# Weight remainders on GpSimd and three seven-product steps in every feed-forward chunk from the third

## The chip, the cores and the metric

One Trainium2 chip, one of its cores. The metric is the device time of one execution in microseconds (us), the median over several runs. Engines: TensorE (PE in the profile, PEld for its weight loads), VectorE (DVE), ScalarE (ACT), GpSimd (POOL), and SyncE (SP), whose queue issues nearly all weight loads.

## The reference

One layer of a decoder on 256 tokens of width 2048, in float32: `x + 1/2 SwiGLU`, `x + Mixer`, `x + 1/2 SwiGLU`, and a last RMSNorm. The change concerns the two feed-forward stages alone:

```python
def rmsnorm(x, g):
    y = x * lax.rsqrt(jnp.mean(x * x, axis=-1, keepdims=True) + EPS)
    return y * g
def swiglu(h, wg, wu, wd):              # wg, wu: 2048 x 5632, wd: 5632 x 2048
    return (jax.nn.silu(h @ wg) * (h @ wu)) @ wd
x = x + 0.5 * swiglu(rmsnorm(x, ffn1_norm), ffn1_wg, ffn1_wu, ffn1_wd)
x = x + hybrid_mixer(rmsnorm(x, mix_norm), ...)
x = x + 0.5 * swiglu(rmsnorm(x, ffn2_norm), ffn2_wg, ffn2_wu, ffn2_wd)
return rmsnorm(x, final_norm)
```

## The kernel before

**Precision.** Every float32 operand is split into a rounded high part and a remainder, both in a format that PE multiplies at full rate. A product is three matmuls: high x high, high x remainder, remainder x high. ScalarE makes the high part of a weight (`w_hi`, line 1305), VectorE the remainder (`w_lo <- raw - w_hi`, `lo`, line 1820).

**Slots.** Weights stream through four buffers. A slot `c` is one load of 512 KB (two k-tiles of 128 rows by 512 columns) into `raw[c % 4]`. ScalarE's `hi` waits until it has landed and until PE has finished slot c - 4; VectorE's `lo` follows; then PE's `group` does 12 matmuls of 128x512 (two k-tiles, two token tiles, three matmuls). SP loads slot c when slot c - 4 has its remainder (`lo_ready`) and, for a PAIR slot, when the weight sums of that step are made (`t_ready`). Each queue serves in order, and no queue skips a waiting instruction.

**Chunks.** A feed-forward stage f has 11 chunks n of 512 of the 5632 columns, 16 slots each: eight for the gate (wg), eight for up (wu). Chunks 0 to 5 are followed by the first part of the down projection, chunks 6 to 10 by the second. Gate results lie in PSUM banks 0 and 1 (one per token tile), up results in banks 2 and 3.

**Seven-product steps.** A PAIR slot (gate weights) and the PAIR2 slot behind it (up weights of the same k-tiles) form one step: the 2x2 block product of two token tiles, two k-tiles and the gate and up columns is done with seven products instead of eight, so with 21 matmuls instead of 24 (`seven_products`). For it VectorE forms four sums of weights in `wt` (`weight_sums`, lines 1882 to 1887), ScalarE splits them (`wt_hi`, line 1356) and VectorE makes their remainders (`wt_low`, line 1892); PAIR2's own remainder is needed for one k-tile only (line 1900). `weight_sums` waits until PE has finished the step before. Some products gather in PSUM banks 4 to 7 and are added to the four banks at the end of a chunk: `product1_copy` (ScalarE, line 1383) copies one bank to `z` when the last step is done, `gate_products` (lines 1957, 1942, 1944, 1959) adds to gate bank 0, forms two sums and adds to gate bank 1, `right_sums` (1950, 1952) forms the sums for up, and `up_products` (1965) adds them when all 16 slots are done.

**Tables.** `CHUNK` holds the slot order of a chunk with two steps, `CHUNK3` that of one with three (at slots 4, 8 and 12); `THREE` lists the chunks that use `CHUNK3`. For chunks in `LATE` the last step ends at slot 13, and the gate sums and SiLUs of chunk n - 1 are done within chunk n's program: ScalarE's `late_silu` behind slots 0 and 1, VectorE's `gate_products` behind slot 0, `right_sums` behind slot 1, `up_products` and `up` (line 2022: SiLU(gate) x up) behind slot 2, and the 32x32 transposes (`gu_transpose`, line 2066) behind slot 3. PE begins chunk n only when both SiLUs of chunk n - 1 have read the gate banks (`silu_done`). GpSimd then issues 16 small DMAs that complete the transposition (`gu_blocks`, line 712), and later slots (9, 10 and 14 with `CHUNK3`, 12 and 13 with `CHUNK`) make the operands of the down projection from them. GpSimd has no other work in these stages.

Of the kernel before, what the change touches and what calls it, by code (L numbers as in the profile page):

```python
# [14 lines left out]
NT = TOK // P  # L15
# [36 lines left out]
         (UP, 0), (UP, 1), (PAIR, 3), (PAIR2, 3), (UP, 4), (UP, 5), (UP, 6), (UP, 7)]  # L52
CHUNK3 = [(GATE, 0), (GATE, 4), (GATE, 5), (GATE, 6), (PAIR, 1), (PAIR2, 1), (GATE, 7), (UP, 0),
          (PAIR, 2), (PAIR2, 2), (UP, 4), (UP, 5), (PAIR, 3), (PAIR2, 3), (UP, 6), (UP, 7)]
THREE = (2, 4, 5, 6, 8, 10)
LATE = (0,) + THREE
H_QUAD = {1: 0, 2: 1, 3: 2}
PAIRS = 2
# [32 lines left out]
def chunk_slot(n):  # L91

    return CHUNK_SLOTS * n + (len(down_job(0)) if n >= PART0[1] else 0)
# [49 lines left out]
def job_no(f, key):  # L143

    return f * len(PAIR_JOBS) + PAIR_JOBS.index(key)
# [10 lines left out]
R_FFN1B, R_CONV, R_ATT, R_FFN2B = range(4)  # L156


def resid(stage, n):

    return NT * (stage * NDC + n + 1)
# [31 lines left out]
AT = {key: MIX0 + n for n, key in enumerate(MIX_ORDER)}  # L193
FFN0 = [0, MIX0 + len(MIX_ORDER)]
END = FFN0[1] + FFN_GROUPS
OUT0 = AT[("out", 1), 0]


# [88 lines left out]
def count(c, i=None, per=0):  # L287

    return c if i is None else i * per + c


def build_program(nc, a, out):
# [170 lines left out]
    with ctx:  # L463
# [3 lines left out]
        landed = [sem(f"landed{s}") for s in range(SLOTS)]  # L467
        hi_ready = sem("hi_ready")
        lo_ready = sem("lo_ready")
        group_done = sem("group_done")  # L470
        x_half_landed = sem("x_half_landed")
        w_half_landed = sem("w_half_landed")
# [126 lines left out]
        def _(sp):  # L599
            def load(c, src, halves=None):  # L600
                if c >= SLOTS:
                    sp.wait_ge(lo_ready, c - SLOTS + 1)
                for f in range(2):
                    if c - SLOTS - FFN0[f] in PAIR_SLOTS:
                        sp.wait_ge(t_ready, pair_no(f, c - SLOTS) + 1)
                s = c % SLOTS
                if halves is None:
                    sp.dma_start(raw[:, s, :, :], src).then_inc(landed[s], 16)
                else:
                    sp.dma_start(raw[:, s, :, 0:CMP_HID], halves[0]).then_inc(landed[s], 16)  # L610
                    sp.dma_start(raw[:, s, :, CMP_HID:CH], halves[1]).then_inc(landed[s], 16)
# [69 lines left out]
        def _(pool):  # L681
# [24 lines left out]
            def gu_blocks(f, n, i=None):  # L706
# [3 lines left out]
                for a_ in range(QB):  # L710
                    for c_ in range(QB):
                        pool.dma_start(gu_raw[c_ * SQ:c_ * SQ + SQ, :, a_, :],  # L712
                                       gu_sq[a_ * SQ:a_ * SQ + SQ, :, c_ * P:c_ * P + P]).then_inc(gu_moved, 16)

            def ffn(f):
                with pool.Fori(0, NFC - 1) as i:
                    gu_blocks(f, 0, i)
                gu_blocks(f, NFC - 1)

            ffn(0)  # L720
            pool.wait_ge(group_done, MIX0)
# [33 lines left out]
        def _(pe):  # L755
            mm = nc.tensor.matmul

            def group(c, i, per, hi, lo, k, banks, first, last, tiles=range(NT), signal=group_done, opened=(), skip=False):


                pe.wait_ge(lo_ready, count(c + 1, i, per))
                s = c % SLOTS
                for kk in range(GK):
                    for t, bank in enumerate(banks):
                        if t not in tiles:
                            continue
                        o = ps[:, bank, :]
                        x_hi = hi[:, k + kk, t * P:t * P + P]
                        x_lo = lo[:, k + kk, t * P:t * P + P]
                        begin = first and kk == 0 and t not in opened  # L770
                        mm(o, x_hi, w_hi[:, s, kk, :], start=begin, stop=False, skip_group_check=skip)  # L771
                        mm(o, x_hi, w_lo[:, s, kk, :], start=False, stop=False, skip_group_check=skip)  # L772
                        ins = mm(o, x_lo, w_hi[:, s, kk, :], start=False, stop=last and kk == GK - 1,  # L773
                                 skip_group_check=skip)
                if signal is not None:
                    ins.then_inc(signal, 1)
# [506 lines left out]
        def _(act):  # L1283
# [143 lines left out]
            def ffn(f):  # L1427
# [24 lines left out]
                def chunk(n, i=None):  # L1452
                    c = FFN0[f] + chunk_slot(n)
                    gu_at = 9 if n in THREE else 12
                    for p, (kind, _) in enumerate(chunk_table(n)):
                        slot(f, c + p, kind, i)
                        if n - 1 in LATE and n != PART0[1] and p < NT:
                            late_silu(f, n - 1, p)
                        if n == 1 and p == 8:
                            hs_high(f, 1)  # L1460
                        if n - 1 not in LATE and p == 0:
                            silu(f, n - 1, i, tiles=(1,))
                        if n != PART0[1]:
                            if p == gu_at:
                                gu_operand(f, n - 1, i)
                            if p == gu_at + 1:
                                gs_high(n - 1, quad_no(f, n - 1), i)
                        if n == PART0[1] and p == 0:
                            product1_copy(f, ("down", 0, 1), c - HALF[0] + last_pair(0, 1))
                        if p == 14 and n not in LATE:  # L1470
                            product1_copy(f, n, c + chunk_pairs(n)[-1], i)
                        if p == 15 and n not in LATE:
                            silu(f, n, i, tiles=(0,))
# [330 lines left out]
        def _(dve):  # L1804
# [10 lines left out]

            def lo(c, i=None, per=0):

                dve.wait_ge(hi_ready, count(c + 1, i, per))
                s = c % SLOTS
                tt(w_lo[:, s, :, :], raw[:, s, :, :], w_hi[:, s, :, :].bitcast(F32),  # L1820
                   ALU.subtract).then_inc(lo_ready, 1)
# [266 lines left out]
            def ffn(f):  # L2088
# [20 lines left out]
                def chunk(n, i=None):  # L2109
                    c = FFN0[f] + chunk_slot(n)  # L2110
                    gu_at = 9 if n in THREE else 12
                    for p, (kind, _) in enumerate(chunk_table(n)):
                        slot(f, c + p, kind, i)
                        if n == PART0[1]:
                            if p in TURN_STEPS:
                                left_residual(f, 0, 1, TURN_STEPS.index(p))
                            if p == 3:
                                right_residual(f, 1)
                        else:
                            if n == 1 and p in (7, 8):  # L2120
                                h_sums(f, 1, p - 7)
                            if n == 1 and p == 9:
                                hs_low(f, 1)
                            if n - 1 in LATE and p == 0:
                                gate_products(f, n - 1)
                            if n - 1 in LATE and p == 1:
                                right_sums(f, n - 1)
                            if p == 2:
                                up_products(f, n - 1, i)
                                up(f, n - 1, i)  # L2130
                            if p == 3:
                                gu_transpose(f, n - 1, i)
                            if p == gu_at:
                                gu_sums(f, n - 1, quad_no(f, n - 1), i)
                            if p == gu_at + 1:
                                gu_operand(f, n - 1, quad_no(f, n - 1), i)
                            if p == (14 if n in THREE else gu_at + 1):
                                gs_low(n - 1, quad_no(f, n - 1), i)
# [510 lines left out]
```

## Time and profile before

| | |
|---|---|
| median of 3 runs | 1814.15 us (1813.94 to 1814.37) |
| span of the profiled execution | 1810.6 us; its own time beyond the span is not given apart |
| PE busy | 1799.3 us (99%) |
| DVE busy | 1555.0 us (86%) |
| ACT busy | 1022.7 us (56%) |
| POOL busy | 246.2 us (14%) |
| DMA, mean rate | 203 GB/s |

The span runs from the first to the last instruction of the profiled execution; a run's time also holds what lies around it. Busy is the time in which an engine executed at least one instruction. A matmul's shown duration (0.39 us) overlaps with the next one's, so the pace of PE is read from starts. In the timelines a row is a start, a duration, the engine, the line of the kernel, the operation, output<-inputs, shapes and a count; with a count over one the duration covers them all.

### The profile page before, as it was taken

To read this page: it belongs to the slowest core of one execution; us is meant where nothing else is said; L and a number is where in the kernel's file an instruction comes from. 1 tells how busy PE (TensorE), PEld (TensorE's weight loads), DVE (VectorE), ACT (ScalarE), POOL (GpSimd) and SP (SyncE) were. 2 spreads that over 40 slices of the span, in tenths; PEclk is the share of its full clock that TensorE was granted. 3 is DMA by queue.
4 is the path that set the end of the run, shared out by engine and by line. 5 is a ranking of instruction groups with operands and counts; after the bars stand their busy time and mean duration, and the time that the engine had idled before them with its cause. 6 is when DMAs were issued, how large, how long until landed. Compare 5 with 4: busy or idle time off the path is not lost.

```text
span 1810.6 us, 21958 instructions
## 1 busy us (share of the span) xinstructions
PE 1799.3 (99%) x8134; PEld 1481.8 (82%) x8134; DVE 1555.0 (86%) x1863; ACT 1022.7 (56%) x1334; POOL 246.2 (14%) x442
## 2 busy tenths in 40 slices
PE   9999999999999999999999999999999999999998
PEld 7788888888888888888788888888888888888886
DVE  7999998889999977678667867899999889999987
ACT  6655555445555556556567745555555455555554
POOL 1111111001111100000123300111111000222100
PEclk9999999999999999999999999999999999999999
DMA  7676766667676766766443655667676666677764
GB/s 244 209 213 221 217 210 211 207 202 220 206 216 203 218 201 207 209 214 194 149 138 107 209 174 185 209 207 218 209 216 212 214 207 194 209 219 221 242 202 151
DMA packets 199289, 367.28 MB, mean 203 GB/s; under 512 B 19013, under 2 KB 23857, under 8 KB 199057
## 3 DMA queue, kind: packets, MB, share of 16 engines
q1 hardware_dynamic: 185008, 352.37, 62.5%
q0 software_dynamic: 11648, 12.02, 2.2%
q10 hardware_dynamic: 2528, 1.52, 0.3%
q8 instruction: 64, 1.05, 0.2%
q14 instruction: 41, 0.33, 0.1%
HBM read 350.11 MB, written 4.19 MB: 196 GB/s over the span
## 4 chain that ended last, share of the span: by engine, by line
PE 93%; DVE 5%; ACT 1%; DMA 1%; issue 0%; ACTq 0%; DVEq 0%
PE ps L771 23%; PE ps L773 23%; PE ps L772 23%; PE ps L789 7%; PE ps L791 7%; PE ps L790 7%; PE ps L838 2%; DVE w_lo L1820 2%; DVE wt_lo L1892 1%; DVE wt L1882 0%; ACT w_hi L1305 0%; PE ps L1069 0%; PE ps L1096 0%; DMA raw<-in_ffn_wu_dram 0%; PE ps L1071 0%
## 5 line engine op out<-in xcount | busy, mean ns | idle before, releaser
L1820 DVE TENSOR_TENSOR w_lo<-raw,w_hi 128x1024 fp32r<-128x1024 f32 x573 | 692.1, 1225 | 111.8 <-ACT w_hi L1305 107.8
L1305 ACT ACTIVATE w_hi<-raw 128x1024 fp32r<-128x1024 f32 x573 | 599.6, 1056 | 287.3 <-PE ps L773 197.8
L771 PE MATMUL ps<-w_hi,hT_hi 128*128 128x512 f32 x1308 | 512.4, 392 | 1.3 <-ACT gu L1399 1.2
L773 PE MATMUL ps<-w_hi,hT_lo 128*128 128x512 f32 x1308 | 509.6, 390 | 0.0
L772 PE MATMUL ps<-w_lo,hT_hi 128*128 128x512 f32 x1308 | 509.3, 389 | 0.0
L712 POOL DMA_DIRECT2D gu_raw<-gu_sq x352 | 187.5, 541 | 1077.2 <-DVE gu_sq L2066 1003.7
L1356 ACT ACTIVATE wt_hi<-wt 128x1024 fp32r<-128x1024 f32 x164 | 172.9, 1054 | 274.7 <-DVE wt L1882 274.7
L771 PEld LDWEIGHTS ps<-w_hi,hT_hi 128*128 128x128 f32 x1308 | 245.7, 188 | 52.0 <-ACT gu L1399 2.1
L773 PEld LDWEIGHTS ps<-w_hi,hT_lo 128*128 128x128 f32 x1308 | 245.6, 188 | 52.0
L772 PEld LDWEIGHTS ps<-w_lo,hT_hi 128*128 128x128 f32 x1308 | 245.7, 188 | 49.7
L1892 DVE TENSOR_TENSOR wt_lo<-wt,wt_hi 128x1024 fp32r<-128x1024 f32 x164 | 199.6, 1217 | 0.0
L771 PE MATMUL ps<-w_hi,guT_hi 128*128 128x512 f32 x496 | 193.0, 389 | 0.0
L773 PE MATMUL ps<-w_hi,guT_lo 128*128 128x512 f32 x496 | 193.0, 389 | 0.0
L772 PE MATMUL ps<-w_lo,guT_hi 128*128 128x512 f32 x496 | 192.9, 389 | 0.0
L1882 DVE TENSOR_TENSOR wt<-raw 128x1024 f32<-128x1024 f32 x82 | 100.0, 1220 | 21.9 <-PE ps L791 10.9
L773 PEld LDWEIGHTS ps<-w_hi,guT_lo 128*128 128x128 f32 x496 | 93.1, 188 | 19.4
L772 PEld LDWEIGHTS ps<-w_lo,guT_hi 128*128 128x128 f32 x496 | 93.1, 188 | 19.3
L771 PEld LDWEIGHTS ps<-w_hi,guT_hi 128*128 128x128 f32 x496 | 93.1, 188 | 19.2
L734 POOL TENSOR_SCALAR prob<-prob,sums,gate 128x128 f32<-128x128 f32 (+1 forms) x64 | 37.3, 593 | 258.7 <-DVE sums L2328 258.7
L789 PE MATMUL ps<-wt_hi,hs_hi 128*128 128x512 f32 x168 | 65.9, 392 | 0.8 <-DVE wt_lo L1892 0.7
L790 PE MATMUL ps<-wt_lo,hs_hi 128*128 128x512 f32 x168 | 65.4, 389 | 0.0
L791 PE MATMUL ps<-wt_hi,hs_lo 128*128 128x512 f32 x168 | 65.4, 389 | 0.0
(312 smaller groups left out, 2219.6 us busy)
## 6 DMA issues: line engine op xcount, KB each, us to landing
raw<-in_ffn_wu_dram SPq DMA_DIRECT2D x176, 512.0 KB, 4.5
raw<-in_ffn_wd_dram SPq DMA_DIRECT2D x176, 512.0 KB, 4.8
raw<-in_ffn_wg_dram SPq DMA_DIRECT2D x175, 512.0 KB, 4.1
raw<-in_w_in_dram SPq DMA_DIRECT2D x88, 512.0 KB, 3.6
raw<-in_w_out_dram SPq DMA_DIRECT2D x32, 512.0 KB, 4.2
gu_raw<-gu_sq POOLq DMA_DIRECT2D x352, 32.0 KB, 3.5
x_parked<-x SPq DMA_DIRECT2D x8, 256.0 KB, 5.3
raw<-in_cmp_k_w_dram SPq DMA_DIRECT2D x8, 256.0 KB, 3.2
```

What stands on the lines that cost most here:

```text
L712: pool.dma_start(gu_raw[c_ * SQ:c_ * SQ + SQ, :, a_, :], gu_sq[a_ * SQ:a_ * SQ + SQ, :, c_ * P:c_ * P + P]).then_inc(gu_moved, 16)
L771: mm(o, x_hi, w_hi[:, s, kk, :], start=begin, stop=False, skip_group_check=skip)
L772: mm(o, x_hi, w_lo[:, s, kk, :], start=False, stop=False, skip_group_check=skip)
L773: ins = mm(o, x_lo, w_hi[:, s, kk, :], start=False, stop=last and kk == GK - 1, skip_group_check=skip)
L789: mm(o, x_hi, y_hi, start=start, stop=False, skip_group_check=True)
L790: mm(o, x_hi, y_lo, start=False, stop=False, skip_group_check=True)
L791: return mm(o, x_lo, y_hi, start=False, stop=stop, skip_group_check=True)
L1305: act.activation(w_hi[:, c % SLOTS, :, :], raw[:, c % SLOTS, :, :], ACT.Copy).then_inc(hi_ready, 1)
L1356: act.activation(wt_hi[:, 2 * half:2 * half + 2, :], wt[:, 2 * half:2 * half + 2, :], ACT.Copy).then_inc(t_hi_ready, 1)
L1820: tt(w_lo[:, s, :, :], raw[:, s, :, :], w_hi[:, s, :, :].bitcast(F32), ALU.subtract).then_inc(lo_ready, 1)
L1882: tt(wt[:, T1:T3 + 1, :], w[:, 2, :].unsqueeze(1).to_broadcast([P, 2, CH]), w[:, 0::3, :], ALU.subtract).then_inc(t1_ready, 1)
L1892: tt(wt_lo[:, sl, :], wt[:, sl, :], wt_hi[:, sl, :].bitcast(F32), ALU.subtract).then_inc(t_lo_ready, 1)
```

## The change

`THREE` grows from chunks 2, 4, 5, 6, 8, 10 to all chunks from 2 to 10, so chunks 3, 7 and 9 now have a third step. In chunks whose predecessor is in `THREE` and that don't open the second part (3, 4, 5, 7, 8, 9, 10: "pooled" chunks), GpSimd makes the remainders of slots 2 and 3 (`remainder`); VectorE only counts them in `lo_ready`. PE, and SP before it reloads the buffer, also wait for `pool_lo`. GpSimd's remainder of slot 2 waits for the first gate sum (`gate_added`), that of slot 3 for the up sums (`prod_used`). In pooled chunks `late_silu` moves from behind slots 0 and 1 to behind slots 1 and 2, and `gate_products` from behind slot 0 to behind slot 1, ahead of `right_sums`.

```diff
-THREE = (2, 4, 5, 6, 8, 10)
+THREE = (2, 3, 4, 5, 6, 7, 8, 9, 10)
+POOLED_AT = (2, 3)
...
+def pooled_chunks():
+    return [n for n in THREE if n - 1 in THREE and n != PART0[1]]
+def pooled_slots():
+    return [FFN0[f] + chunk_slot(n) + p for f in range(2) for n in pooled_chunks() for p in POOLED_AT]
...
# SP, load
                 sp.wait_ge(lo_ready, c - SLOTS + 1)
+                if c - SLOTS in POOLED:
+                    sp.wait_ge(pool_lo, POOLED.index(c - SLOTS) + 1)
...
# POOL
+            def remainder(f, n, p):
+                c = FFN0[f] + chunk_slot(n) + p
+                s = c % SLOTS
+                pool.wait_ge(hi_ready, c + 1)
+                if p == POOLED_AT[0]:
+                    pool.wait_ge(gate_added, 2 * (NFC * f + n - 1) + 1)
+                else:
+                    pool.wait_ge(prod_used, job_no(f, n - 1) + 1)
+                pool.tensor_tensor(w_lo[:, s, :, :], raw[:, s, :, :], w_hi[:, s, :, :].bitcast(F32),
+                                   ALU.subtract).then_inc(pool_lo, 1)
             def ffn(f):
-                with pool.Fori(0, NFC - 1) as i:
-                    gu_blocks(f, 0, i)
-                gu_blocks(f, NFC - 1)
+                for n in range(NFC):
+                    if n in pooled_chunks():
+                        for p in POOLED_AT:
+                            remainder(f, n, p)
+                    if n and n != PART0[1]:
+                        gu_blocks(f, n - 1)
+                    if n == PART0[1] - 1 or n == NFC - 1:
+                        gu_blocks(f, n)
...
# PE, group
                 pe.wait_ge(lo_ready, count(c + 1, i, per))
+                if c in POOLED:
+                    pe.wait_ge(pool_lo, POOLED.index(c) + 1)
...
# ACT, chunk
-                        if n - 1 in LATE and n != PART0[1] and p < NT:
-                            late_silu(f, n - 1, p)
+                        at_ = p - (n in pooled_chunks())
+                        if n - 1 in LATE and n != PART0[1] and 0 <= at_ < NT:
+                            late_silu(f, n - 1, at_)
...
# DVE, lo and chunk
+                if c in POOLED:
+                    dve.sem_inc(lo_ready, 1)
+                    return
...
-                            if n - 1 in LATE and p == 0:
+                            if n - 1 in LATE and p == (1 if n in pooled_chunks() else 0):
                                 gate_products(f, n - 1)
```

## Rows read from the trace of the kernel before

**Rows 1.** Page, part 1: busy us (share of the span) xinstructions.
```profile
PE 1799.3 (99%) x8134; PEld 1481.8 (82%) x8134; DVE 1555.0 (86%) x1863; ACT 1022.7 (56%) x1334; POOL 246.2 (14%) x442
```
**Rows 2.** Timeline of PE, chunk 4, stage 1: start us, us, engine, line.
```profile
193.12 0.39 PE L789 MATMUL ps<-w_hi,hT_hi 128*128 128x512 f32 x1
...
197.88 0.39 PE L771 MATMUL ps<-w_hi,hT_hi 128*128 128x512 f32 x1
...
203.32 0.39 PE L789 MATMUL ps<-w_hi,hT_hi 128*128 128x512 f32 x1
```
**Rows 3.** Windows: chunk 4, stage 1, busy time of PE, PEld, DVE, ACT, POOL; clock; DMA.
```profile
182.20:223.70 41.50, 41.50 (x184) 34.35 (x184) 39.58 (x46) 24.00 (x27) 8.51 (x16) 1.00 0.70 214
```
**Rows 4.** Groups by line and form, DVE: busy us, mean ns, idle before.
```profile
L1820 DVE TENSOR_TENSOR w_lo<-raw,w_hi 128x1024 fp32r<-128x1024 f32 x573 | 692.1, 1225 | 111.8 <-ACT w_hi L1305 107.8
L1892 DVE TENSOR_TENSOR wt_lo<-wt,wt_hi 128x1024 fp32r<-128x1024 f32 x164 | 199.6, 1217 | 0.0
L1882 DVE TENSOR_TENSOR wt<-raw 128x1024 f32<-128x1024 f32 x82 | 100.0, 1220 | 21.9 <-PE ps L791 10.9 <-DMA raw<-in_ffn_wu_dram 8.3 <-DMA raw<-in_ffn_wd_dram 2.7
```
**Rows 5.** Timeline of DVE, start of chunk 5, stage 1.
```profile
226.77 1.41 DVE L2022 SCALAR_TENSOR_TENSOR gu<-ps,rs,gu 128x512 f32<-128x512 f32 x2
...
230.45 1.18 DVE L1820 TENSOR_TENSOR w_lo<-raw,w_hi 128x1024 fp32r<-128x1024 f32 x1
...
237.01 3.48 DVE L1820 TENSOR_TENSOR w_lo<-raw,w_hi 128x1024 fp32r<-128x1024 f32 x3
```
**Rows 6.** Timeline of POOL and DVE in the mixer.
```profile
1025.33 1.46 POOL L744 TENSOR_TENSOR uT<-uT 128x512 f32<-128x512 f32 x1 [5.82 <-ACT uT L1649]
1029.19 3.19 POOL L748 TENSOR_TENSOR att_sq<-att_sq 128x1024 f32<-128x1024 f32 x1
...
1025.67 0.42 DVE L2341 TENSOR_TENSOR p_q<-ps,shifted 64x256 f32<-64x256 f32 x1
...
1027.81 2.32 DVE L1820 TENSOR_TENSOR w_lo<-raw,w_hi 128x1024 fp32r<-128x1024 f32 x1
```
**Rows 7.** Timeline of SP, DVE, ACT and PE, turn 2-3, stage 1.
```profile
131.22 5.51 SPq L608 DMA_DIRECT2D raw<-in_ffn_wg_dram  x4
...
136.25 0.69 DVE L1957 TENSOR_TENSOR ps<-ps,z 128x512 f32<-128x512 f32 x1
...
139.09 0.69 ACT L1399 ACTIVATE gu<-ps,rs 128x512 f32<-128x512 f32 x1 [0.41 <-DVE ps L1959]
...
140.08 0.39 PE L771 MATMUL ps<-w_hi,hT_hi 128*128 128x512 f32 x1
```
**Rows 8.** DMA issues, windows 131:132, 1230:1231, 213:215; last number: us to landing.
```profile
raw<-in_ffn_wg_dram SPq DMA_DIRECT2D x1, 512.0 KB, 4.5
...
raw<-in_ffn_wg_dram SPq DMA_DIRECT2D x1, 512.0 KB, 4.2
...
raw<-in_ffn_wg_dram SPq DMA_DIRECT2D x1, 512.0 KB, 4.0
```
**Rows 9.** Timeline of DVE, ACT and PE, turn 2-3, stage 2.
```profile
1235.17 0.69 DVE L1957 TENSOR_TENSOR ps<-ps,z 128x512 f32<-128x512 f32 x1
...
1238.01 0.69 ACT L1399 ACTIVATE gu<-ps,rs 128x512 f32<-128x512 f32 x1 [0.41 <-DVE ps L1959]
...
1238.75 0.50 PE L771 MATMUL ps<-w_hi,hT_hi 128*128 128x512 f32 x1
```
**Rows 10.** Timeline of DVE, ACT and PE, chunk 4 and turn 4-5, stage 1.
```profile
198.86 1.23 DVE L1882 TENSOR_TENSOR wt<-raw 128x1024 f32<-128x1024 f32 x1 [1.34 <-DMA raw<-in_ffn_wu_dram]
...
213.53 0.68 DVE L1900 TENSOR_TENSOR w_lo<-raw,w_hi 128x512 fp32r<-128x512 f32 x1
...
219.27 0.69 DVE L1957 TENSOR_TENSOR ps<-ps,z 128x512 f32<-128x512 f32 x1
...
222.11 0.69 ACT L1399 ACTIVATE gu<-ps,rs 128x512 f32<-128x512 f32 x1 [0.40 <-DVE ps L1959]
...
223.72 0.39 PE L771 MATMUL ps<-w_hi,hT_hi 128*128 128x512 f32 x1
```

More of the change, by code:

```diff
@@ L195 @@
 END = FFN0[1] + FFN_GROUPS
+POOLED = pooled_slots()
 OUT0 = AT[("out", 1), 0]
@@ L469, in build_program @@
         lo_ready = sem("lo_ready")
+        pool_lo = sem("pool_lo")
         group_done = sem("group_done")
```

## The prediction

> **What bounds the kernel now.** I read the page's busy times first: TensorE (PE) is busy 1799.3 of 1810.6 us [rows 1]. So time falls only if PE gets fewer matmuls, and rises by whatever PE is made to wait. The timeline of PE gives the price of a matmul: a seven-product step starts at 193.12 and the slot behind it at 197.88, which is 4.76 us for 21 matmuls, 0.2267 us each; the two plain slots that follow take 5.44 us for 24 [rows 2]. A step saves three matmuls, 0.68 us. The windows by chunk show the second-busiest engine: VectorE (DVE) is busy 39.58 of the 41.5 us of chunk 4, a chunk of three steps [rows 3]. So DVE has some 2 us of room per chunk, and the rows at the turns between chunks decide whether PE waits.
>
> **Removed from PE.** Chunks 3, 7 and 9 go from two steps to three, in both feed-forward stages: 6 steps x 3 x 0.2267 = 4.08 us. The number of slots and bytes stays.
>
> **DVE's balance.** A step more costs DVE one whole remainder less (a PAIR2 slot has half a one) and, more, the weight sums and two wt_lo. By the durations [rows 4] the two wt_lo are 2 x 1.22; the sums are one of 1.22 and two of half that width, the remainder left in PAIR2 another half, some 0.65 each; less the whole remainder of 1.22 that is +4.4 us, 4.2 at the pitch of 1.13 at which such instructions follow each other (three in 3.48 us, [rows 5]). The two pooled remainders give back 2.3 us. Chunks 3, 7 and 9 thus load DVE with 1.9 us more than now, chunks 4, 5, 8 and 10 with 2.3 less; chunk 2 and chunk 6 stay unrelieved. Since chunk 4 already lives with three steps and no relief at 39.58 of 41.5 us, a pooled chunk of three steps, at about 37.3, has room. I cost this at nothing on PE. With the third step these chunks also take the transposed product of the chunk before at slots 9, 10 and 14 instead of 12 and 13; chunk 4 does that now, and [rows 3] shows PE busy all through it.
>
> **POOL's remainder.** No row shows this operation. The nearest: L748, a POOL sum of 128x1024 f32, shown as 3.19 us; but DVE's L1820 beside it stretches from 1.22 to 2.32 and ends at 1030.13, and L748 ends at 1032.38, so each had waited for the other and POOL's own work was 2.25 us [rows 6]. Bounds: 1.46 us (L744, half the width, with a short overlap) and 3.19 us. I take 2.25. With a PSUM input DVE is not touched: L2341 (p_q<-ps,shifted) ran in its 0.42 us inside L744's 1025.33 to 1026.79. So what counts is that no DVE instruction with two SBUF inputs falls beside the remainders. The first waits for the gate's first sum and for ScalarE's w_hi of slot 2 and lies beside the remaining product sums, which all read PSUM. The second waits for prod_used, the start of `up`: from there to slot 4's remainder DVE takes 230.45 - 226.77 = 3.68 us now, 2.55 without slot 3's remainder [rows 5]. 2.25 us fit, by 0.3; at 3.19 they would hold slot 4's remainder 0.6 us, which then is still 0.5 earlier than now. PE's new waits stand ahead of the matmuls of slots 2 and 3 and all that follows. PE needs slot 3 only 8.2 us into the chunk and slot 2 at 5.4, so POOL has over 3 us to spare there; the loads of slots 6 and 7 wait for POOL too and start about when they start now. On POOL's queue the 16 DMAs of gu_blocks stand behind the second remainder; they wait for the transposes anyway, which end later.
> The Trainium skill (SBUF — State Buffer, "SBUF: two separate sides") says the port pair that the two engines share is locked whole by a GpSimd operation or by a DVE one with two SBUF inputs, so that the loser stands still. The stretched L1820 agrees. It speaks against the offload in general, and by it a second remainder that starts 0.3 us late would hold slot 4's remainder on DVE by as much.
>
> **The moved gate sums: here the time goes.** PE starts a chunk only when both SiLUs of the chunk before are done (gate banks). Now the chain at a turn is: pair end, copy z, gate sum, two product sums, second gate sum, second SiLU. Before the copy ScalarE does one w_hi of the new chunk, before the gate sum DVE one remainder (slot 0). After the change in pooled chunks it is two: slot 1's w_hi and remainder too. ScalarE and DVE serve in order, so slot 1's load has become part of the chain; it can be issued only when slot 13 (PAIR2) of the chunk before has its half remainder.
> Turn of chunk 2 to 3, stage 1 [rows 7, 8]: this load is issued at 131.22 and takes 4.5 us, so it lands at 135.7. w_hi of slot 1 then runs 135.8 to 136.8 (1.06), the copy z to 137.4, the remainder 136.9 to 138.0, and the gate sum starts at 138.0 where it now starts at 136.25. All behind it moves by 1.77: the second SiLU, now 139.09 to 139.78, ends at 141.55. PE now starts the chunk at 140.08, a slack of 0.3; it waits 1.5 us. Nothing upstream helps, since chunk 2 has no pooled slots.
> The same turn in stage 2 [rows 8, 9]: the one load issued between 1230 and 1231, at the earliest moment (1230.1, behind slot 13's half remainder), takes 4.2 us and lands at 1234.3; w_hi to 1235.4, remainder 1235.5 to 1236.6; gate sum at 1236.6 for 1235.17, +1.45. PE already starts on the SiLU's heels there (1238.75 after 1238.01 + 0.69), so it waits 1.45 us more. Together 2.96 us.
> At the other turns into pooled chunks (3-4, 4-5, 7-8, 8-9, 9-10) the chunk before is itself pooled and DVE is earlier. From the turn 4-5 [rows 10]: DVE begins the second pair's sums at 198.86; with two remainders fewer it could be 2.3 earlier, but it must wait for the pair before to end on PE, at 197.88 [rows 2], which leaves a lead of 1.0. From there it works without a gap, so slot 13's half remainder comes at 212.5 for 213.53, the load (4.0 us here, [rows 8]) is issued 0.7 later and lands at 217.2, w_hi ends at 218.3, the remainder at 219.5 and the gate sum starts at 219.5 for 219.27: +0.25, and the second SiLU ends at 223.05 before PE's 223.72. No wait, with 0.6 to spare; a load 0.7 us slower would use it up. The turn 6-7 has its load early (half remainder some 11 us ahead of the chunk). I add 0.1 us in all for single slow loads.
>
> **Sum.** 1810.6 - 4.08 + 2.96 + 0.1 = 1809.6, so -1.0 on the span. The median of the runs is 1814.15, 3.5 us above the profiled span, which I keep: 1813.1 us.
>
> **Rivals.**
> - *The moved sums cost nothing* (slot 1's load is in time, or the SiLU had room): -4.08, 1810.1. For it: PE hardly waits anywhere now. Against: a slack of 0.3 and 0.05 us at the two turns, and a landing that no part of the change brings forward. 10%.
> - *The second remainder starts behind `up`* because `up` reads gu and the scalar rs from SBUF: it then ends 1.4 us later, slot 4's remainder comes where it comes now, and DVE's lead of 1.0 at the last pair is gone. The load lands at 218.2, its w_hi ends at 219.3, and the second SiLU at about 224.0 against 223.72: 0.3 us at each of ten turns, 3 us: 1816. L2341 has an SBUF input and no scalar, so the rows don't exclude it. 14%.
> - *Slower: the remainders and DVE exclude each other in `up` and in the transposes too.* Place: the start of each of the 14 pooled chunks. POOL gets in only behind the transposes, and slot 4's remainder stands for 2.25 us: DVE is 1.1 us later than now instead of 1.0 earlier, and slot 1's load with it. The second SiLU would end 1.4 us late; a late start of a chunk gives DVE up to half of that back, so I take 1.0 us at each of ten turns: 1813.1 + 10 = 1823. It decides once slot 4's remainder comes later than now. The stretched L1820 speaks for exclusion, L2341 against one by a PSUM reader; the transpose has a single input and no row beside POOL. 13%.
> - *The forecast*: 63%, from 1811.5 to 1814.5.
>
> A measurement of this kernel tells about 0.2%, 3.6 us, from no change, so faster is under 1810.5 and slower over 1817.8. Faster is the first rival: 10%. Slower is the last one and a tail of the second: 14%. The rest, 76%, is the same. The range takes in the first rival at its lower end and the second with its tail, and leaves out the last: 1810.0 to 1817.6.
>
> **What would show it.** PE idle 1.4 to 1.6 us ahead of chunk 3 in both stages, released by the SiLU (L1399's line), and none over 0.3 at the other turns; POOL's remainders at 2.2 to 2.4 us; DVE's remainder of slot 4 at 1.22 us, not stretched; w_hi of slot 1 ended by its DMA at the turn 2-3; 18 matmuls fewer. Wrong would be: no PE wait at the turn 2-3 (first rival), stretched w_lo behind the transposes (last), or POOL remainders over 3 us.

## The result, and the profile after

| | median, us | lowest to highest | runs |
|---|---|---|---|
| before | 1814.67 | 1812.35 to 1816.62 | 19 |
| changed | 1818.39 | 1814.92 to 1821.89 | 19 |

The ratio is 1.0024, 95% interval 1.0017 to 1.0030: 3.7 us slower, where 1.0 us faster was forecast. The range ended at 1817.6. A later measurement of the same two kernels (experiment 3) gave 1821.16 against 1813.71 (1.0043, 1.0029 to 1.0056). The profiled execution spans 1818.0 us (before 1810.6) and took 1819.8 by its own time. Every run of which both are on record lies 1.8 us over its span, so the profiled execution of before took about 1812.4: it was 2.3 under its kernel's median, and that of the changed kernel 1.4 over. The spans therefore differ by 7.4, the medians by 3.7.

Three lines of the page after: busy times (they answer to [rows 1]), the chain that ended last by engine, and the group of POOL's new operation.
```profile
PE 1800.5 (99%) x8116; PEld 1478.5 (81%) x8116; DVE 1553.4 (85%) x1865; ACT 1030.2 (57%) x1346; POOL 313.2 (17%) x470
...
PE 77%; DVE 16%; DMA 4%; ACT 2%; issue 1%; ACTq 0%; DVEq 0%; SPq 0%
...
L739 POOL TENSOR_TENSOR w_lo<-raw,w_hi 128x1024 fp32r<-128x1024 f32 x28 | 67.2, 2402 | 627.1 <-ACT w_hi L1339 322.5
```
PE has 18 matmuls fewer, as said. Its busy time says little by itself, since a matmul that follows a wait is shown longer. The chain says more: a fifth of the span now runs over DVE and DMAs, 6% before. PE's waits, from the view of waits (us in total, times, longest), name where it stands:
```profile
PEld ps L805 <- ACT gu L1433: 12.4, 12, 2.2
...
PE ps L805 <- ACT gu L1433: 7.5, 9, 1.8
```
L1433 is the SiLU (L1399 before). The same rows before:
```profile
PEld ps L771 <- ACT gu L1399: 2.1, 2, 1.6
...
PE ps L771 <- ACT gu L1399: 1.2, 1, 1.2
```
One of these waits, 1.3 us at the turn 0-1 of stage 1, stands in every kernel here, and the sums below leave it out.

**Turn 2-3, stage 1**, timeline of SP, ACT, DVE and PE (start, duration, engine, line, [idle before <-releaser]); it answers to [rows 7].
```profile
133.04 0.37 SPq L623 DMA_DIRECT2D raw<-in_ffn_wg_dram  x1
...
137.88 1.06 ACT L1339 ACTIVATE w_hi<-raw 128x1024 fp32r<-128x1024 f32 x1 [1.68 <-DMA raw<-in_ffn_wg_dram]
...
138.97 1.23 DVE L1858 TENSOR_TENSOR w_lo<-raw,w_hi 128x1024 fp32r<-128x1024 f32 x1 [0.81 <-ACT w_hi L1339]
...
140.12 0.69 DVE L1995 TENSOR_TENSOR ps<-ps,z 128x512 f32<-128x512 f32 x1
...
142.95 0.69 ACT L1433 ACTIVATE gu<-ps,rs 128x512 f32<-128x512 f32 x1 [0.42 <-DVE ps L1997]
...
143.69 0.50 PE L805 MATMUL ps<-w_hi,hT_hi 128*128 128x512 f32 x1 [1.77 <-ACT gu L1433]
...
144.03 0.40 PE L806 MATMUL ps<-w_lo,hT_hi 128*128 128x512 f32 x1
```
The chain is the forecast one: DMA, w_hi of slot 1, remainder, gate sum, SiLU, PE. From here on a turn's times are counted from the moment at which PE would have started the chunk, 5.44 us (24 matmuls) behind the end of the last pair; here that is 141.77. PE waits 1.93 us. The last pair ends at 136.33 in this run.

**The same turn in stage 2** (it answers to [rows 9]); undelayed start 1244.39, wait 1.50.
```profile
1240.08 1.06 ACT L1339 ACTIVATE w_hi<-raw 128x1024 fp32r<-128x1024 f32 x1 [1.21 <-DMA raw<-in_ffn_wg_dram]
...
1245.90 0.50 PE L805 MATMUL ps<-w_hi,hT_hi 128*128 128x512 f32 x1 [1.34 <-ACT gu L1433]
```

**Turn 4-5, stage 1** (it answers to [rows 10]), timeline and, from the view of DMA issues for window 216.8:217.1, the landing of slot 1's load, which is issued at 216.92. Undelayed start 227.08.
```profile
201.24 0.39 PE L805 MATMUL ps<-w_hi,hT_hi 128*128 128x512 f32 x1
...
201.54 1.23 DVE L1920 TENSOR_TENSOR wt<-raw 128x1024 f32<-128x1024 f32 x1 [1.08 <-PE ps L825]
...
216.20 0.68 DVE L1938 TENSOR_TENSOR w_lo<-raw,w_hi 128x512 fp32r<-128x512 f32 x1
...
222.08 1.06 ACT L1339 ACTIVATE w_hi<-raw 128x1024 fp32r<-128x1024 f32 x1 [1.81 <-DMA raw<-in_ffn_wg_dram]
...
224.31 0.69 DVE L1995 TENSOR_TENSOR ps<-ps,z 128x512 f32<-128x512 f32 x1
...
227.15 0.69 ACT L1433 ACTIVATE gu<-ps,rs 128x512 f32<-128x512 f32 x1 [0.41 <-DVE ps L1997]
...
227.88 0.50 PE L805 MATMUL ps<-w_hi,hT_hi 128*128 128x512 f32 x1 [0.64 <-ACT gu L1433]
```
```profile
raw<-in_ffn_wg_dram SPq DMA_DIRECT2D x1, 512.0 KB, 5.1
```
Here none was forecast, and PE waits 0.80. The load took 5.1 us, where [rows 8] have 4.0 for the same load before. The first two rows are the last pair's weight sums and the PE slot whose start lies just ahead of them; the row at 216.20 is the half remainder.

Where slot 1's landing is what the chain waits for, it has one length: the second SiLU ends 5.78 us behind the landing of slot 1's load (0.03 to w_hi, 1.09 to the remainder, 1.14 to the gate sum, 2.84 to the SiLU, 0.69 for it), and PE starts 0.05 later. The one exception is the turn 8-9 of stage 1: 6.06 here and 6.05 in the second profile, because the second SiLU starts 0.28 later behind its gate sum there; why is not shown. So the wait can be worked out from the landing. All turns of the profiled run (us from the undelayed start):

| turn | half remainder, st. 1 / 2 | load took | landed | PE waits |
|---|---|---|---|---|
| 2-3 | -9.44 / -9.15 | 4.81 / 4.11 | -3.91 / -4.33 | 1.93 / 1.50 |
| 3-4 | -10.88 / -10.87 | 4.46 / 4.16 | -5.70 / -6.00 | 0.14 / 0 |
| 4-5 | -10.88 / -10.87 | 5.14 / 4.82 | -5.03 / -5.34 | 0.80 / 0.50 |
| 7-8 | -10.88 / -10.87 | 4.26 / 4.57 | -5.91 / -5.58 | 0 / 0.26 |
| 8-9 | -10.87 / -10.87 | 5.12 / 4.89 | -5.04 / -5.27 | 1.07 / 0.57 |
| 9-10 | -10.88 / -10.88 | 5.01 / 4.84 | -5.15 / -5.33 | 0.68 / 0.51 |

The turn 6-7 is moved too and has no wait (landed -6.64 / -6.35). The waits of the table sum to 7.96 us; before it was 0.22, at the turn 2-3 of stage 2. Each wait costs 0.11 us more: the first matmul behind it starts 0.34 us before the second (143.69, 144.03), where 0.227 is the rule.

**What became of POOL.** Timeline of POOL and DVE at the start of chunk 5, stage 1 (DVE's rows answer to [rows 5]):
```profile
226.82 2.38 POOL L739 TENSOR_TENSOR w_lo<-raw,w_hi 128x1024 fp32r<-128x1024 f32 x1 [27.62 <-ACT w_hi L1339]
229.85 2.41 POOL L739 TENSOR_TENSOR w_lo<-raw,w_hi 128x1024 fp32r<-128x1024 f32 x1 [0.65 <-DVE ps L2003]
```
```profile
229.74 1.41 DVE L2060 SCALAR_TENSOR_TENSOR gu<-ps,rs,gu 128x512 f32<-128x512 f32 x2
231.18 1.30 DVE L2104 STREAM_TRANSPOSE gu_sq<-gu 128x512 f32<-128x512 f32 x2
232.41 1.18 DVE L1858 TENSOR_TENSOR w_lo<-raw,w_hi 128x1024 fp32r<-128x1024 f32 x1
```
Nothing on DVE is stretched, and POOL ends at 232.26, before slot 4's remainder. All 28 of them are like that. Two of the rivals, "behind `up`" and the exclusion in `up` and in the transposes, are out by these rows.

**The ledger of the span**, 7.4 us: matmuls -4.08, waits +7.74, restarts +1.1 (ten of them, one before). That is 4.8. Another +1.7 is there before the first pair ends (at 51.03, before 49.35). That is not the change: the second profile of the changed kernel has 49.52 there, and one of a kernel that is faster than both has 51.11. About 1.0 is not placed.

### The profile page after: what moved, and what is told of

Read it like the earlier page. It is cut to its first block, busy times and chain, and to the rows that moved or that the text cites. A ratio compares the mean times of both kernels' runs of the same rounds, so it can differ in the third digit from the quotient of the medians.

```text
span 1818.0 us, 22026 instructions
## 1 busy us (share of the span) xinstructions
PE 1800.5 (99%) x8116; PEld 1478.5 (81%) x8116; DVE 1553.4 (85%) x1865; ACT 1030.2 (57%) x1346; POOL 313.2 (17%) x470
## 4 chain that ended last, share of the span: by engine, by line
PE 77%; DVE 16%; DMA 4%; ACT 2%; issue 1%; ACTq 0%; DVEq 0%; SPq 0%
PE ps L805 19%; PE ps L807 19%; PE ps L806 19%; PE ps L823 5%; PE ps L825 5%; PE ps L824 5%; DVE w_lo L1858 4%; DMA raw<-in_ffn_wg_dram 2%; DVE wt_lo L1930 2%; DVE wt L1920 2%; PE ps L872 2%; ACT w_hi L1339 1%; DVE wt L1923 1%; DVE wt L1925 1%; DVE w_lo L1938 1%
## 5 line engine op out<-in xcount | busy, mean ns | idle before, releaser
L1858 DVE TENSOR_TENSOR w_lo<-raw,w_hi 128x1024 fp32r<-128x1024 f32 x539 | 653.1, 1227 | 111.8 <-ACT w_hi L1339 106.0
L805 PE MATMUL ps<-w_hi,hT_hi 128*128 128x512 f32 x1260 | 495.1, 393 | 7.8 <-ACT gu L1433 7.5
L807 PE MATMUL ps<-w_hi,hT_lo 128*128 128x512 f32 x1260 | 491.0, 390 | 0.0
L806 PE MATMUL ps<-w_lo,hT_hi 128*128 128x512 f32 x1260 | 490.7, 389 | 0.0
L1390 ACT ACTIVATE wt_hi<-wt 128x1024 fp32r<-128x1024 f32 x176 | 185.5, 1054 | 285.1 <-DVE wt L1920 285.1
L805 PEld LDWEIGHTS ps<-w_hi,hT_hi 128*128 128x128 f32 x1260 | 236.7, 188 | 60.9 <-ACT gu L1433 12.4
L807 PEld LDWEIGHTS ps<-w_hi,hT_lo 128*128 128x128 f32 x1260 | 236.5, 188 | 50.5
L806 PEld LDWEIGHTS ps<-w_lo,hT_hi 128*128 128x128 f32 x1260 | 236.7, 188 | 47.4
L1930 DVE TENSOR_TENSOR wt_lo<-wt,wt_hi 128x1024 fp32r<-128x1024 f32 x176 | 214.5, 1219 | 0.0
L739 POOL TENSOR_TENSOR w_lo<-raw,w_hi 128x1024 fp32r<-128x1024 f32 x28 | 67.2, 2402 | 627.1 <-ACT w_hi L1339 322.5
```

Source lines behind the costliest of these rows:

```text
L1390: act.activation(wt_hi[:, 2 * half:2 * half + 2, :], wt[:, 2 * half:2 * half + 2, :], ACT.Copy).then_inc(t_hi_ready, 1)
L1930: tt(wt_lo[:, sl, :], wt[:, sl, :], wt_hi[:, sl, :].bitcast(F32), ALU.subtract).then_inc(t_lo_ready, 1)
```

## The experiments

All in five rounds, beside the kernel before on the same chip. "Gate sums" stands for DVE's two sums into the gate banks with the product sums between them, "SiLUs" for ScalarE's copy z and the two SiLUs.

**1. Gate sums and SiLUs at their old slots; POOL's remainders and the third steps kept.**
```diff
-                        at_ = p - (n in pooled_chunks())
+                        at_ = p
-                            if n - 1 in LATE and p == (1 if n in pooled_chunks() else 0):
+                            if n - 1 in LATE and p == 0:
```


> The changed kernel with the gate sums and SiLUs back behind slots 0 and 1; GpSimd's remainders and the third steps stay. Theory A (slot 1's load has become part of the chain at a turn: in the trace of the changed kernel the second SiLU ends 5.78 us behind that landing at every turn into a pooled chunk): the eleven waits of 8 us in all go, only the saving of 18 matmuls is left, 4.1 us under the kernel before, and PE waits nowhere over 0.3 us at turns 2-3 to 9-10. Rival B (GpSimd's remainders delay VectorE or the loads, wherever the sums stand): the waits stay, the time is 2 to 5 us over before. GpSimd's first remainder should now start about 0 us at the chunk's start instead of -1, and its second end at 4.8 and hold slot 4's remainder on VectorE by some 0.7 us.

1810.29 us against 1814.33 (ratio 0.9980, 0.9971 to 0.9989), 11 runs. PE waits 0.12 and 0.21 us at the two turns 2-3 and, but for the turn 0-1, nowhere else behind a SiLU. Timeline of DVE, ACT, POOL and PE at the turn 4-5, stage 1:
```profile
220.34 0.70 DVE L1995 TENSOR_TENSOR ps<-ps,z 128x512 f32<-128x512 f32 x1 [0.43 <-ACT z L1417]
...
223.18 0.69 ACT L1433 ACTIVATE gu<-ps,rs 128x512 f32<-128x512 f32 x1 [0.42 <-DVE ps L1997]
224.90 4.77 POOL L739 TENSOR_TENSOR w_lo<-raw,w_hi 128x1024 fp32r<-128x1024 f32 x2 [27.39 <-ACT w_hi L1339]
...
229.58 1.18 DVE L1858 TENSOR_TENSOR w_lo<-raw,w_hi 128x1024 fp32r<-128x1024 f32 x1
```
The second SiLU ends at 223.87, 1.1 us before the chunk (224.95). Since ScalarE makes slot 2's w_hi behind it, POOL starts its two remainders only at 224.90, back to back, beside DVE's sums of PSUM, and ends at 229.67, 0.09 into slot 4's remainder, which shows its usual 1.18 (all 14 cases are alike); the 0.7 us of delay that the expectation gave it did not come. So the move was not needed to keep the two engines apart. The whole loss, and more, lies in it; this kernel beats both.

**2. The same again, on the chip of the second measurement of the changed kernel.**

> The changed kernel with gate sums and SiLUs at their old slots, again, beside the changed kernel on one chip. Theory A (the moved sums are the whole loss): 7 to 9 us under the changed kernel and 3 to 5 under the kernel before; PE waits at the two turns 2-3 alone, by 0.3 us at most. Rival: the first measurement fell on a favourable chip, and the two come within 3 us of each other.

1810.67 against 1813.71 (0.9980, 0.9971 to 0.9989), 11 runs; the waits are 0.21 and 0.09 at the turns 2-3, none elsewhere. Over both measurements that makes 3.0 to 4.0 us less than before, where -4.08 for the matmuls and +0.1 to 0.2 for the turn 2-3 were to be expected.

**3. The changed kernel, second measurement.**

> The changed kernel itself, on the same chip as the two others. All theories: 0.2 to 0.35% above the kernel before. What it tells is whether the waits at the turns keep their places and sizes in a second profile: 1.9 and 1.5 us at the turns 2-3, 0 to 1.1 at the others, and whether slot 1's load again takes 4.2 to 5.2 us.

1821.16, 0.43% over the kernel before and 10.5 us over the kernel of experiment 2 beside it, 5 runs; both are more than was expected. Waits of 1.40 and 2.10 us at the turns 2-3 and 0 to 0.85 at the others, 6.5 in all; the same load took 4.25 to 4.92 us. The landings differ; landed + 5.78 gives each wait but that of the turn 8-9 of stage 1. What is new is in the windows around the 2.10 (us, busy times of PE, PEld, DVE, ACT, POOL; granted clock, DMA share, GB/s):
```profile
1240.70:1242.80 2.10, 0.16 (x2) 0.00 (x1) 2.03 (x4) 1.68 (x3) 1.07 (x1) 1.00 0.96 349
...
1244.00:1246.00 2.00, 2.00 (x6) 1.52 (x6) 1.97 (x3) 0.00 (x0) 1.33 (x2) 0.50 0.34 48
```
After PE had stood idle, the granted clock was 0.50, the 1.2 GHz level; most matmuls were 0.43 us apart instead of 0.227, and nine of them from 1243.37 on took 1.6 us more than at the full clock. In the first profile no wait was followed by this. The mean clock of the runs fits: it is 0.998 in all five runs here and in five of the 19 of the first measurement (median 1820.6), and 0.999 in the other 14 (1818.2) and in all 27 of the kernel before beside this one. The median of this measurement lies 2.7 us over its own profiled run (1818.48), so other executions lost more; where is not shown.

**4. Only the move: the kernel before, with gate sums and SiLUs one slot later in chunks 3, 5, 7 and 9.**
```diff
+MOVED = (3, 5, 7, 9)
...
-                        if n - 1 in LATE and n != PART0[1] and p < NT:
-                            late_silu(f, n - 1, p)
+                        at_ = p - (n in MOVED)
+                        if n - 1 in LATE and n != PART0[1] and 0 <= at_ < NT:
+                            late_silu(f, n - 1, at_)
...
-                            if n - 1 in LATE and p == 0:
+                            if n - 1 in LATE and p == (1 if n in MOVED else 0):
```


> The kernel before with one edit: at the turns into chunks 3, 5, 7 and 9 the SiLUs stand behind slots 1 and 2 and the gate sums behind slot 1. No GpSimd work, no third step added. Theory A with the landings of the trace of before (-4.34, -5.48, -6.97, -5.28 us from the undelayed chunk start in stage 1, -4.22, -6.04, -6.80, -5.52 in stage 2) and 5.78 us of chain: waits of 1.4, 0.3, 0, 0.5, 1.3, 0, 0, 0.3, with 0.1 for each restart of PE +4.4 us, 0.24% over before. Rival B: no change.

1821.41 against 1814.33 (1.0042, 1.0028 to 1.0055): +7.1, more than the 4.4 worked out. View of waits:
```profile
PEld ps L772 <- ACT gu L1400: 11.0, 7, 2.7
PE ps L772 <- ACT gu L1400: 8.1, 7, 2.3
```
Waits at the four turns: 1.85, 1.03, 0, 0.40 in stage 1 and 2.48, 0.69, 0, 1.40 in stage 2. The move costs by itself, without POOL and without a matmul less. It cost more than expected because the expectation took the landings from the trace of before, where slot 1's load took 3.93 to 4.67 us at these eight turns; it took 4.42 to 5.04 here.

**5. The changed kernel without POOL's remainders; sums and SiLUs still moved.**
```diff
-POOLED_AT = (2, 3)
+POOLED_AT = ()
```


> Third steps, no remainders on GpSimd (VectorE makes all), gate sums where the pooled list is empty, so at their old places: identical to e3 by its code, kept as its repeat. Theory A: -4 to +1 us against before. Rival B: -4 us, since no GpSimd work is left.

1835.50 against 1814.33 (1.0120, 1.0104 to 1.0135), 4 runs; the profiled one, 1832.18, is the fastest of them. The expectation misread its own edit: the list of chunks does not depend on POOLED_AT, so the sums stay moved, and this is no "three steps alone". Read as what it is, it isolates the relief by POOL under the move:
```profile
PE ps L805 <- ACT gu L1433: 16.8, 13, 2.2
```
With DVE unrelieved the half remainder comes at -9.2 to -10.5 instead of -10.9 (at the turns 3-4, 4-5, 7-8, 8-9 and 9-10), the load with it, and the waits behind turn 0-1 sum to 17.5 us instead of 8.0. Behind two of the waits, 2.15 and 1.98 us, the clock fell to its lower level, as in experiment 3; that is part of the time too. The relief was worth 17 us to the changed kernel.

**6. The third steps alone: no POOL, sums and SiLUs at their old slots** (the edits of 1 and 5 together).
```diff
-POOLED_AT = (2, 3)
+POOLED_AT = ()
...
-                            if n - 1 in LATE and p == (1 if n in pooled_chunks() else 0):
+                            if n - 1 in LATE and p == 0:
```

> Third steps in chunks 3, 7, 9 alone: VectorE makes all remainders, gate sums at their old places (the kernel before with the longer THREE). It takes the offload away from e1. Theory A's account of VectorE: 42.4 us of work at its pitch in a three-step chunk against 41.5 on PE, so 0.9 us too much in each of the chunks that follow one another, less the 1 us of slack at the turns: PE waits of 0 to 0.9 us at turns 3-4, 4-5, 8-9, 9-10, released by a SiLU or a wt_lo, and 0 to +5 us against before in all; e1 is faster than it by 4 to 9 us. If the offload were worth nothing (the third rival turned round), it equals e1, -4 us.

1819.76 against 1814.08 (1.0036, 1.0022 to 1.0050), 5.7 us more where 0 to 5 was expected. View of waits, then chunk 4 in the windows (it answers to [rows 3]):
```profile
PEld ps L823 <- DVE wt_lo L1930: 9.8, 23, 0.9
```
```profile
183.00:224.60 41.60, 41.45 (x181) 33.20 (x180) 40.04 (x48) 22.65 (x26) 8.50 (x16) 1.00 0.71 208
```
The waits that are new stand inside the chunks, not at the turns as expected: the second halves of the weight sums are late, and DVE is busy 40.04 of 41.6 us. Beside experiment 1 the two remainders on POOL are worth 9.5 us; this is what lets three steps pay in a row of chunks.

**7. Only ScalarE's order moved: gate sums back at slot 0 on DVE, SiLUs one slot late.**
```diff
-                            if n - 1 in LATE and p == (1 if n in pooled_chunks() else 0):
+                            if n - 1 in LATE and p == 0:
```


> The changed kernel with only VectorE's half of the move taken back: gate_products behind slot 0 again, ScalarE's copy and SiLUs still behind slots 1 and 2. Slot 1's landing and w_hi stay in the chain, slot 1's remainder leaves it, so the second SiLU ends 5.15 us behind the landing instead of 5.78. Theory A: with landings of -4.0 at turns 2-3 and -5.0 to -6.0 at the others the waits are 1.1 at each 2-3 and 0 to 0.15 elsewhere, 2.5 us in all with the restarts of PE: -1 to -2 us against before. If VectorE's remainder alone made the waits: -4 us. If ScalarE's order alone did: as the changed kernel, +3.7 us.

1827.77 against 1814.08 (1.0075, 1.0061 to 1.0089): +13.7 where 1 to 2 less was expected. Timeline of POOL and DVE at the start of chunk 3, stage 1:
```profile
142.95 2.37 POOL L739 TENSOR_TENSOR w_lo<-raw,w_hi 128x1024 fp32r<-128x1024 f32 x1 [27.11 <-ACT w_hi L1339]
143.09 3.31 DVE L1858 TENSOR_TENSOR w_lo<-raw,w_hi 128x1024 fp32r<-128x1024 f32 x1
```
and, behind PE's wait of 1.96 us there, the window of its first matmuls (granted clock 0.65):
```profile
144.00:148.00 4.00, 3.98 (x12) 3.12 (x13) 3.86 (x4) 0.91 (x1) 1.32 (x1) 0.65 0.11 15
```
DVE's remainder of slot 1 stands until POOL is done at 145.32 and then runs its 1.1 us. DVE ends the chunk 1 to 2 us later, the half remainder falls to -9.1, the next load with it, and PE waits 0.95 to 2.0 us at six of the ten turns 3-4, 4-5, 7-8, 8-9 and 9-10. The clock fell behind two of its waits. The profiled run, 1834.96, is the slowest of the five. My expectation had left out what the moved gate sums also do: they put DVE's slot-1 remainder ahead of POOL's first.

**8. As 7, with POOL's first remainder released by DVE's remainder of slot 1.**
```diff
-                    pool.wait_ge(gate_added, 2 * (NFC * f + n - 1) + 1)
+                    pool.wait_ge(lo_ready, c)
```


> The kernel of the scalar move alone (gate sums at slot 0 of DVE's order, SiLUs one slot late), with one edit: POOL's first remainder waits for DVE's remainder of slot 1 instead of the first gate sum. Theory A: what made that kernel slow (1827.8) is the meeting of POOL's first remainder with DVE's of slot 1, which stood 3.3 to 3.4 us instead of 1.22. Then here DVE's slot-1 remainder is back at 1.2 us, POOL's stays at 2.4, the half remainder at the chunk's end comes at about -10.5 to -10.9 us again, the second SiLU ends 5.15 us after slot 1's landing (w_hi of slot 1 is still ahead of it on ScalarE, the remainder not), and PE waits 1 to 2 us at the two turns 2-3 and at most 0.4 at the others: 1811 to 1815, 13 to 17 us less than without the edit. Theory B: the order of ScalarE's work alone costs this, whatever POOL meets: it stays above 1822.

1817.13 against 1813.71 (1.0017, 1.0008 to 1.0026), 11 runs: 10.6 us less than 7, though 2 us over the range expected.
```profile
143.10 1.21 DVE L1858 TENSOR_TENSOR w_lo<-raw,w_hi 128x1024 fp32r<-128x1024 f32 x1
...
144.47 2.40 POOL L739 TENSOR_TENSOR w_lo<-raw,w_hi 128x1024 fp32r<-128x1024 f32 x1 [28.16 <-DVE w_lo L1858]
```
The meeting is gone, and with it most of 7's loss. What is left are waits of 5.8 us, up to 0.92 at the turns behind 2-3 where at most 0.4 was expected: w_hi of slot 1 still stands ahead of the copy z on ScalarE.

**9. The changed kernel with the sums of chunk 2 back at their old slots, in chunk 3 alone.**
```diff
-                        at_ = p - (n in pooled_chunks())
+                        at_ = p - (n in pooled_chunks() and n != 3)
-                            if n - 1 in LATE and p == (1 if n in pooled_chunks() else 0):
+                            if n - 1 in LATE and p == (1 if n in pooled_chunks() and n != 3 else 0):
```


> The changed kernel with gate sums and SiLUs of chunk 2 back at their old slots in chunk 3 alone (both stages); the other five pooled turns per stage stay moved. Theory A: the loss is a sum over turns, each its own. Then the waits of 1.93 and 1.50 us at the turns 2-3 and the two restarts of 0.11 go, and the others stay (4.5 us in all): 3.0 to 3.8 us less than the changed kernel's run on this chip. Rival B: a wait at turn 2-3 delays PE and so gives DVE and the loads time; without it the next turns wait longer, and less than 1.5 us is won. Rival C: the loss is mainly at turn 2-3, through what it starts, and the time comes to that of the kernel with all sums back (about 8 us less).

1815.60 (1812.27 to 1816.82, 11 runs) against 1821.16 beside it: 5.6 us less by medians, more than the 3.0 to 3.8 expected, with 4.2 us of waits left. By the spans of the profiled runs, without the uneven start, it is 3.6, for 2.3 less of waits and the 1.6 of the slow stretch of experiment 3. Rival B, under 1.5 us won, is out, though it holds in a small part: without the wait at 2-3 the half remainder of the turn 3-4 comes at -10.36 and -10.71, where it was -10.88 and -10.87. The ten later turns wait 3.9 us in all, between the 4.5 and 3.0 of the two profiles that have the wait at 2-3. Rival C is out too: the kernel with all sums back is another 4.9 us faster. So the turns add up, near enough.

**10. The kernel of experiment 1 with POOL at slots 10 and 11, behind its DMAs.** DVE also waits for its own earlier remainders before it counts a pooled one.
```diff
-POOLED_AT = (2, 3)
+POOLED_AT = (10, 11)
...
+                    dve.wait_ge(lo_ready, c)
                     dve.sem_inc(lo_ready, 1)
```


> e1 with GpSimd's two remainders at slots 10 and 11 of the pooled chunks, behind its small DMAs, instead of at slots 2 and 3: there VectorE's instructions have two SBUF inputs. It measures what the place beside the PSUM sums is worth. If the two engines shut each other out (third rival's mechanism, here without its PSUM cover): w_lo, wt and wt_lo beside a remainder take up to 3.6 us instead of 1.22, GpSimd's remainders 3 to 4 us instead of 2.40, VectorE loses 4.8 us per pooled chunk and saves 2.3, PE waits at most turns and the time is 5 to 25 us over e1. If they don't: as e1, -4 us against before.

1856.37 against 1814.08 (1.0235, 1.0221 to 1.0249). Timeline of POOL and DVE in chunk 4, stage 1, and the waits:
```profile
212.06 2.42 POOL L739 TENSOR_TENSOR w_lo<-raw,w_hi 128x1024 fp32r<-128x1024 f32 x1 [7.64 <-ACT w_hi L1339]
212.17 2.47 DVE L2080 TENSOR_TENSOR gs<-gs,gu_raw 128x128 f32<-128x128 f32 x1
```
```profile
PE ps L805 <- POOL w_lo L739: 20.0, 19, 2.3
```
A sum of 128x128 with two SBUF inputs, 0.28 us otherwise, stands for 2.47; weight sums come to 3.41. The loss is 46 us over experiment 1, nearly twice the upper end of what was expected, for the same two remainders: PE also waits for POOL itself, 20.0 us as shown, and 3.1 us for the count on DVE's queue. Which share is whose was not separated.

## Why the prediction was wrong

**Right:** the price of the removed matmuls. With the move taken away they come back as 3.0 to 4.0 us (experiments 1 and 2), for 4.08 less the 0.1 that the turns 2-3 wait longer than before.

**Right:** POOL's part. 2.40 us for 2.25; `up` and the transposes unstretched; both remainders inside their gaps; that they cost PE nothing is shown by experiment 1, whose PE has no wait from them. The Trainium skill (SBUF — State Buffer, "SBUF: two separate sides") lets only a DVE operation in a 2-port mode or with two SBUF inputs and a GpSimd one shut each other out; experiments 7 and 10 show it with 3.31 and 2.47 us, and the 28 cases beside PSUM readers and transposes show its other side. The Trainium skill also says that moving work between these two engines "might not help" (Perfetto Trace Analysis, "Optimizing Scalar/DVE Operations"); that fits experiment 10 (1856.37), while in experiment 1 (1810.29, against 1819.76 in 6) it did help.

**Right in mechanism:** slot 1's load joins the chain. At the turn 2-3 of stage 2 the forecast was 1.45 us more than now and 1.28 came (1.50 for 0.22). In stage 1 it was 1.5 and 1.93 came: the load took 4.81 us for 4.5, and its issue was 0.14 later (-8.72 for -8.86).

**The step that failed** is, in its words, "No wait, with 0.6 to spare" at the turns 3-4, 4-5, 7-8, 8-9 and 9-10. Two of its numbers were off.

The first is the issue. The half remainder came at -10.88, not at 212.5 - 223.72 = -11.2, and within 0.01 us at all ten turns. The prediction let the last pair's weight sums begin with PE's next slot; they begin 0.30 us behind its start (201.54 and 201.24). From there to the half remainder it is 14.66 us, and was 14.67 before (213.53 - 198.86), so PE sets this place and DVE's lead beyond it no longer helps.

The second is the load, taken at 4.0 us, the row of the one turn I worked out. With -10.16 for the issue and 5.78 for the chain, the break-even is a load of 4.38 us; by the prediction's own numbers it was 4.7 ("a load 0.7 us slower would use it up"). At these ten turns the load took 4.16 to 5.14, mean 4.73, and in the second profile 4.25 to 4.92, mean 4.58. The trace of before has 22 loads issued right behind a turn's last half remainder, 3.93 to 5.17 with a mean of 4.45; ten of them are slot 1's gate weights as here, mean 4.32. So the 4.0 was near its fast end. A fast load gives nothing back while a slow one costs in full: over the 22, ten turns cost 0.5 us in all by a break-even of 4.67, and 1.7 by 4.38. The text priced this at 0.1. It cost 4.5 in the first profile and 3.0 in the second. The rest is that the loads were slower than in the trace of before, whose ten turns have a mean of 4.44; in the eleven other profiles here it is 4.52 to 4.75. What makes one load slower than the next, and whether that one profile was a fortunate one, is not shown.

**Not in the sum at all:** the restart of 0.11 us per wait, 1.1 us, and the clock's fall to its lower level behind a wait, 1.6 us in one profile and none in the other. The 3.5 us between span and median, which the prediction kept, are 1.8 of every run and a profiled execution of before that was fast; they do not bear on the difference of the two kernels. That the runs of the changed kernel spread over 7.0 us and those of before over 4.3 fits waits that hang on DMA landings; it was not shown by itself.

**The rivals:** "the moved sums cost nothing" is refuted by experiments 1 and 4. The second and the third gave the times nearest to the result (1816 and 1823) by mechanisms that do not occur. The true one, slot 1's load at all turns, was not among them as a rival, though it is one term of the forecast.

## What to carry to other kernels

When a reordering puts a DMA's landing into a chain that had none, price it with the whole spread of that transfer's durations in the trace, not with the row of the turn being worked out: one-sided waits add up. Here that would have given 1.7 us with the right issue time, of the 3.0 to 4.5 that came, so leave room above it. Of an edit that does two things (relieve an engine, and make room for the relief), ask of each whether the other needs it; here the relief was worth 9.5 us and the room made for it cost 8.1 to 10.5. Before giving POOL a part of DVE's work, list what DVE does beside it: the same two remainders made PE wait nowhere beside sums of PSUM, and the kernel that had them beside sums of SBUF, in the middle of a chunk, was 46 us slower.

## What was not expected of the hardware

- The same 512 KB load, issued at the same point of the schedule, took 3.9 to 5.3 us from turn to turn and run to run.
- A DVE instruction with two SBUF inputs that starts beside POOL's remainder stands for its whole rest: 3.31 us for 1.22, 3.41 for 1.21, 2.47 for 0.28. One that reads PSUM (0.68, 0.69, 0.75, 1.23) or a transpose (0.71) is not touched, with the same POOL operation beside it.
- PE's first matmul behind a wait costs 0.11 us more, and behind the wait of 2.10 us the granted clock was 0.50 for most of nine matmuls. Over the profiles of this case PE waited thirteen times for 1.9 to 2.5 us; the clock fell behind five of these waits (1.96, 1.98, 1.98, 2.10, 2.15) and not behind the other eight, of which the longest was 2.48.
